# Second query/key groups and half of the mixing linear are placed among 24 uses of score banks

## The reference, cut to what matters

```python
qa, ka, va, qb, kb, vb = even_project(h_lat, w_in, q_gain, k_gain)   # one matrix w_in
qa = apply_rope(qa, cos, sin); ka = apply_rope(ka, cos, sin)
ya, ya_c = global_gqa(qa, ka, va, qa_c, ka_c, va_c, ctx_out)         # the first 8 heads
yb, yb_c = neighbourhood_attention(qb, kb, vb, qb_c, kb_c, vb_c, rpb, ctx_out)  # 8 more
y_lat = jnp.concatenate([ya, yb], -1) @ w_out                        # the mixing linear
x_lat = layer_norm(DN_ALPHA * x_lat + m_lat[2] * y_lat, ...)
```

## Time and profile before

| | |
|---|---|
| three runs | 2612.84, 2616.89, 2617.99 us |
| median | 2616.89 us |
| the profiled execution, first to last instruction | 2617.9 us |
| mean granted clock of TensorE | 0.990 |
| PE busy, DVE busy, ACT busy | 95%, 62%, 49% of the span |
| first to last matmul of the attention and its start of mixing | 147.27 to 261.44 us |

### The profile page before, as it was taken

The page is one execution under the profiler, slowest core; times in us unless marked ns, Lnnn a source line. Parts: engine busy times, 40 slices in busy tenths (PEclk is TensorE's granted clock), DMA queues, the critical chain, the costliest instruction groups (busy, mean ns, idle before and its releaser), DMA issues.

```text
span 2617.9 us, 41421 instructions
## 1 busy us (share of the span) xinstructions
PE 2496.8 (95%) x15930; PEld 2086.0 (80%) x15930; DVE 1616.8 (62%) x2600; ACT 1271.2 (49%) x2348; POOL 253.3 (10%) x266
## 2 busy tenths in 40 slices
PE   7998999999988999999999999899999999999998
PEld 4865778888956999889886687688889899778887
DVE  2646565553677786668776763533325798775664
ACT  3355454433657665544326743422225644675553
POOL 3000100001202100305000001000002430011000
PEclk9999999999999999999999999999999999999999
DMA  8256522224555555534424434532235555634555
GB/s 282 88 207 205 193 89 97 97 88 133 163 167 198 162 183 170 172 119 146 126 93 151 154 124 169 209 96 96 91 94 167 165 182 169 199 115 138 188 176 150
DMA packets 137893, 393.56 MB, mean 150 GB/s; under 512 B 13776, under 2 KB 40400, under 8 KB 137616
## 3 DMA queue, kind: packets, MB, share of 16 engines
q1 hardware_dynamic: 135872, 386.47, 45.9%
q0 software_dynamic: 1872, 5.02, 0.7%
HBM read 390.39 MB, written 1.05 MB: 150 GB/s over the span
## 4 chain that ended last, share of the span: by engine, by line
PE 80%; DVE 8%; ACT 5%; DMA 4%; issue 2%; POOL 1%; SPq 0%; ACTq 0%; DVEq 0%; POOLq 0%
PE bank L722 20%; PE bank L723 20%; PE bank L724 20%; PE bank L719 4%; PE bank L770 2%; DVE w_low L2065 2%; PE bank L718 2%; ACT w_high L1312 1%; PE bank L937 1%; DMA ring<-in_w_mod 1%; PE bank L950 1%; DMA ring<-in_w_down 1%; PE bank L910 1%; PE bank L912 1%; PE bank L911 1%
## 5 line engine op out<-in xcount | busy, mean ns | idle before, releaser
L2065 DVE TENSOR_TENSOR w_low<-ring,w_high 128x1024 fp32r<-128x1024 f32 (+2 forms) x604 | 689.2, 1142 | 519.8 <-ACT w_high L1312 517.4
L722 PE MATMUL bank<-h_high,w_high 128*128 128x512 f32 (+1 forms) x2576 | 883.9, 343 | 36.5 <-DVE h_low L2262 7.9
L724 PE MATMUL bank<-h_high,w_low 128*128 128x512 f32 (+1 forms) x2576 | 869.7, 338 | 0.0
L723 PE MATMUL bank<-h_low,w_high 128*128 128x256 f32 (+1 forms) x2432 | 821.2, 338 | 0.0
L1312 ACT CAST w_high<-ring 128x1024 fp32r<-128x1024 f32 (+2 forms) x604 | 574.1, 953 | 284.2 <-DMA ring<-in_w_down 147.7
L722 PEld LDWEIGHTS bank<-h_high,w_high 128*128 128x128 f32 x2576 | 493.0, 191 | 98.7 <-issue 25.1
L724 PEld LDWEIGHTS bank<-h_high,w_low 128*128 128x128 f32 x2576 | 493.1, 191 | 50.6
L723 PEld LDWEIGHTS bank<-h_low,w_high 128*128 128x128 f32 x2432 | 464.7, 191 | 49.5 <-issue 1.7
L722 PE MATMUL bank<-f_high,w_high 128*128 128x256 f32 (+1 forms) x616 | 194.9, 316 | 4.3 <-DVE w_low L2065 3.8
L724 PE MATMUL bank<-f_high,w_low 128*128 128x256 f32 (+1 forms) x616 | 193.0, 313 | 0.0
L723 PE MATMUL bank<-f_low,w_high 128*128 128x256 f32 (+1 forms) x528 | 168.1, 318 | 0.0
(11 more groups left out here) (323 smaller groups left out, 3515.9 us busy)
## 6 DMA issues: line engine op xcount, KB each, us to landing
ring<-in_w_up SPq DMA_DIRECT2D x176, 512.0 KB, 3.4
ring<-in_w_mod SPq DMA_DIRECT2D x112, 512.0 KB, 4.6
ring<-in_w_down SPq DMA_DIRECT2D x80, 384.0 KB, 3.1
ring<-in_w_down SPq DMA_DIRECT2D x80, 320.0 KB, 3.0
spare_slabs<-in_w_mod SPq DMA_DIRECT2D x48, 512.0 KB, 7.9
ring<-in_w_gate SPq DMA_DIRECT2D x48, 512.0 KB, 3.4
ring<-in_w_k SPq DMA_DIRECT2D x32, 512.0 KB, 3.5
ring<-in_w_v SPq DMA_DIRECT2D x32, 512.0 KB, 3.5
```

The lines of the kernel that those rows point to most:

```text
L722: pe.matmul(out, wh[:, cols], high, start=first, stop=False)
L723: pe.matmul(out, wh[:, cols], low, start=False, stop=False)
L724: ins = pe.matmul(out, wl[:, cols], high, start=False, stop=last)
L2065: v.tensor_tensor(wl[:, cols], raw[:, cols], wh[:, cols].bitcast(F32), ALU.subtract).then_inc(low_ready, 1)
```

## The change

ev_qk is cut: its first 5 groups stay, then ev_v, and the 8 groups for the second heads (ev_qk_b) are done inside the first heads' attention. mix1_0 is cut by rows of w_out: mix1_0_a takes the first heads' 4 chunks (8 groups of 12 matmuls, half slabs of 0.26 MB) inside the second heads' attention, and its product is added to X there; mix1_0 keeps the second heads' 4 chunks. The attention is counted in 24 uses of two score banks each (three banks, 2, 3 and 4, in turn; bank 1 is free for the woven linears). The lists QK_AT, MIX_AT and MODS_AT say at which use a linear's group and how many modulation slabs stand, and SP loads in that order (`Woven`). Head norm and rope of the first heads move under the last ev_qk and the ev_v groups, the masking of the bias moves into uses 2, 5, 7 and 8, and part 1_0_1 is turned and stored at use 12. Probabilities of uses 0 to 11 go to parts of the qk space, outputs of the first heads to other space. Instruction lists of other layers stay as they are.

```diff
+USES = 24
+QK_AT = [3 * c + i for c in range(4) for i in range(2)]
+MIX_AT = list(range(15, 23))
+MODS_AT = [3] + [2] * 11 + [3] * 3 + [1, 2, 2] * 2 + [1, 1, 2]
...
-            plan += [Linear("ev_qk", 13, [8], TOK, "scalar"), Linear("ev_v", 5, [8], TOK, "scalar")]
+            plan += [Linear("ev_qk", 5, [8], TOK, "scalar"), Linear("ev_v", 5, [8], TOK, "scalar")]
+            qk = Linear("ev_qk_b", 8, [8], TOK, "scalar", source="ev_qk", skip=5, bank=1)
+            qk.opens = 1
+            mix = Linear("mix1_0_a", 8, [4], TOK, "scalar", source="mix1_0", bank=1)
...
+            for s in range(USES):
+                entries += [(L, at.index(s)) for L, at in ((qk, QK_AT), (mix, MIX_AT)) if s in at]
+                entries += [next(slabs) for _ in range(MODS_AT[s])]
...
+            def woven_load(L, k):
...
+                sp.wait_ge(slab_done, L.places[k] - (RING - 1))
...
+            def attend_uses(name, beside):
...
+                scores(0)
+                for s in range(A.uses):
+                    if s + 1 < A.uses:
+                        scores(s + 1)
+                    beside(s)
+                    turn(s)
+                    if s:
+                        values(s - 1)
+                values(A.uses - 1)
...
+                        for k in range(first, first + MODS_AT[s]):
+                            if k and k % 16 == 0:
+                                pe.wait_ge(rows_copied, rows_before + k // 16)
+                            mod_slab(BESIDE["block1"][k // 16], k % 16)
...
+                exps(0)
+                for s in range(A.uses):
+                    if s + 1 < A.uses:
+                        exps(s + 1)
+                    cast(s + 1)
+                    beside(s)
+                    copy(s)
...
+                    def next_cast(s):
+                        if s in QK_AT[1:]:
+                            ahead((At(LIN["ev_qk_b"], QK_AT.index(s), QK_AT.index(s) % RING, None), 0))
+                        elif s in MIX_AT:
+                            ahead((At(LIN["mix1_0_a"], MIX_AT.index(s), MIX_AT.index(s) % RING, None), 0))
+                        elif s == USES - 1:
+                            begin(LIN["mix1_0"], ahead, (0,))
...
+                        done = sum(MODS_AT[:s + 1]) // 16
+                        if done > sum(MODS_AT[:s]) // 16:
+                            mod_copy(BESIDE["block1"][done - 1])
...
+                maxima(0)
+                for s in range(A.uses):
+                    normalise(s)
+                    if s >= 2 and A.last(s - 2):
+                        store(A.owner[s - 2])
+                    if s + 1 < A.uses:
+                        maxima(s + 1)
+                    cast(s + 1)
+                    beside(s)
...
```

349 lines of the change are left out of this document (291 added, 58 removed).

## The result

| | before | after |
|---|---|---|
| median of the runs on this chip | 2616.61 us | 2642.62 us (2637.48 to 2645.52) |
| ratio, with 95% interval | 1 | 1.0099 [1.0081, 1.0118] |
| profiled execution, first to last instruction | 2617.9 | 2643.7 |
| end of the last value turn to first matmul of mix1_0 (attention) | 114.2 | 196.8 |
| less the woven matmuls in it (8 x 5.44 + 8 x 2.72 = 65.3) | 114.2 | 131.5 |

A forecast was written before the change was run, and what follows sets the result against it. PE was taken to bound the linears, with 18.8 us excess over work in the attention. 2617.9 - 18.8 + 19.9 + 5.8 = 2624.8 profiled, 2623.8 as median, less 1 for overlap: 2622.8 us (+5.9), range 2611 to 2632.

The forecast's parts named there:

- new waits in the attention: Waits of PE named one by one, from the start through uses 1 to 14 to the end: sum 15.0 us.
- half clock in the attention: PE at 1.2 GHz behind waits: two drops, 3.4 us as before; 5.1 if the wait at use 1 counts too.
- bursts and borders: More bursts of slabs (24 for 15) and 16 more borders of groups in the attention: 0 to 3, taken as 1.5 us.
- excess of before that goes: Attention of 114.2 us less PE's own work of 95.4: 18.8 us, all won if nothing takes its place.
- mixing linear, half clock left out: End of the mixing linear: last gates stand behind late up slabs, residual at T+30.8 for T+25.0; 5.8 us.
- use 1: Second woven group in the attention: its weights are asked for only when group 0 ends, so PE waits 2.0 us.
- use 14: Slab 32 needs second-part rows that ACT copies behind use 15's exponentials and a cast: PE waits 3.9 us.
- end: End of attention: ACT's cast of the first second-half slab in use 22 holds DVE's norming of use 23; 3.4 us.
- DMA keeps up: Rival, mixing linear: up slabs land before PE ends group 6, the 5.8 falls to 0 to 2; 2617 to 2619; chance 0.18.
- Groups cover everything: Rival, uses 14 and 1: those waits and one clock drop go, about 2610 us with a short mixing wait; chance 0.12.
- DVE becomes the bound: Rival, attention uses 2, 5, 8 and 12 to 14: 1 to 2 us at six uses, 2629 to 2633; chance 0.22.
- It does not do what it says: Rival, attention: each woven group waits for its weights by about what it hides; 2615 to 2620 us; chance 0.06.

The follow-up runs named there:

- b: Changed kernel with slabs per use in uses 12 to 20 altered, so slab 31 ends use 14 and slab 32 starts use 15; ratio 1.0072 to the kernel before.
- k: Changed kernel with mixing linear whole, only query/key groups woven, other slabs per use, first mixing slab cast behind the last turned copies; ratio 1.0003.
- h: Changed kernel with mix1_0 one linear of 8 groups of 24 matmuls again, query/key groups still woven; ratio 1.0049 to the kernel before.
- e: Changed kernel with cures for every named wait joined, and casts at uses 3, 6 and 9 put ahead of exponentials and maxima; ratio 1.0058.
- l_up_ahead: As i, but of eleven spare slabs two load behind mixing slab 4, three behind slab 7 and six behind the second up slab; ratio 1.0010.
- d_gate_before_cast: Changed kernel with gate and residual of mix1_0 groups 6 and 7 ahead of cast and w_low of the two up slabs; ratio 1.0075.
- o_qk_only_spread: As l_up_ahead with its slabs per use, but mixing linear whole and only query/key groups woven; ratio 0.9989 to the kernel before.
- g: Changed kernel with the order of d_gate_before_cast, and of eleven spare slabs two loaded behind mixing slab 4, nine behind slab 7; ratio 1.0082.
- j: As g, but both gates and residuals of mix1_0 groups 6 and 7 ahead of both casts of the up slabs; ratio 1.0086.
- i: As e, but casts of uses 3, 6 and 9 behind exponentials and maxima again, and both last gates and residuals ahead of both up-slab casts; ratio 1.0034.
- a: Changed kernel with the second woven query/key group directly behind the first, use 0's three modulation slabs moved into use 1; ratio 1.0082.
- c: Changed kernel with mix1_0's first half-slab cast moved from use 22 behind use 23's turned copies, its w_low behind use 23's norming; ratio 1.0092.
- f: Changed kernel with mix1_0's first slab cast behind use 23's turned copies, its w_low between the last two stores; ratio 1.0065.

## Why the prediction was wrong

Of the signs that would show it wrong one came true: the attention less the woven groups is 131.5 where it should have been near 115. Everything from the first matmul of ev_qk on, against the steps of the prediction:

| term | predicted | measured |
|---|---|---|
| new waits in the attention | 15.0 | 18.7 |
| half clock in the attention | 3.4 | 8.9 |
| bursts and borders | 1.5 | 8.5 |
| excess of before that goes | -18.8 | -18.8 (kept, so that the rest adds up) |
| mixing linear, half clock left out | +5.8 | +7.3 |
| half clock in the mixing linear 2.1, norm longer by 1.2 (half clock 1.7) | 0 | +3.3 |
| ahead of the attention | 0 | -1.9 |
| overlap | -1 | |
| sum | +5.9 | +26.1 |

**Which way, and the chain of reasons: right.** Each wait that I named is there in its place, for the cause named, and the waits for modulation slabs are gone.

**Waits: right in kind, 3.7 short.** Start 1.8 (2.4), use 1 3.35 (2.0), uses 3, 6 and 9 1.8 (2.6), use 7 0.5 (0.7), use 14 4.4 (3.9), end 6.0 (3.4), and 0.8 for a slab that I hadn't counted. Both large misses are a slab's time to land. At use 1 I took 3.0 from the end of a group to its cast and it was 4.4 (issued 112.49, cast 116.87); at the end 1.8 for a half slab alone in the queue and it was 4.9 (issued 283.38, cast 288.27). In b the same half slab took 2.7. Why a transfer of this size takes now 2.7 and now 4.9 is open.

**The clock: the step that failed most.** I kept the 3.4 of before since 1.50 alone had brought no drop, and charged two drops at 1.7; it was 8.9 in the attention and 12.7 in all, 9.3 more. The profiles of all kernels here hold 39 waits of PE of 2.0 us and more between 100 and 345 us, and in or within 1.5 us behind 35 of them began a stretch at 1.2 GHz; at the 278 shorter ones there are five such stretches more (at 1.86 in k, 1.85 in h, 1.31 and 0.96 in e, and at 1.15 and 0.68 close together in the kernel before). And a drop does not always cost 1.7: at the waits of the changed kernel it was 3.1, 3.0, 5.0 and, in the norm, 1.7. So a wait of 4 us is one of 7. The prediction also works the clock out with the wait at use 1 counted, by the Trainium skill, TensorE: Matmul & The Clock Gate, on HAM oscillation. That section states that a wait which lets the clock fall is paid again each time it recurs; whether a wait of 2.0 does so was my addition. The waits at this place were longer, 3.35 to 4.17 us, and each brought a drop, so three drops was the right count in the attention. The 5.1 was still too little, as it kept the price.

**Bursts and borders: the step that failed next, and that none of the cures brings back.** My 95.4 for PE's own work was low, and 1.5 for the new borders lower. It shows in PE's timeline at one woven half group of the changed kernel:

```profile
244.79 1.13 PE L1037 MATMUL bank<-big 64*128 64x512 f32 x4
245.85 0.50 PE L820 MATMUL bank<-o_halves,w_high 128*128 128x512 f32 x1
246.19 0.40 PE L821 MATMUL bank<-o_halves,w_high 128*128 128x512 f32 x1
246.43 0.40 PE L822 MATMUL bank<-o_halves,w_low 128*128 128x512 f32 x1
...
248.51 0.39 PE L822 MATMUL bank<-o_halves,w_low 128*128 128x512 f32 x1
248.83 1.05 PE L871 MATMUL bank<-ring,cvec_padded 128*8 128x256 f32 x16
```

From its first matmul to the next is 0.34, from its last to the slabs 0.32, between 0.23. A half group takes 2.98 where I counted 2.72, a whole one 5.66 for 5.44: 8 x 0.25 + 8 x 0.22 = 3.8. The values of a use alone take 1.02 where two uses in a row took 1.9, 24 x 0.07 = 1.7; slabs in twos 0.49 each for 0.47, 1.0; scores 24 x 1.06 and 0.9 more at their start, where I had 24.5: 1.8; turns take 1.02, 0.5 less in all than I had. That is 7.8 of the 8.5 measured (131.5 - 18.7 - 8.9 = 103.9, less 95.4). l_up_ahead shows the same number with nothing else in it: no half clock, 7.0 of waits, and 176.5 - 65.3 - 7.0 = 104.2 of work. In the kernel before it was 114.2 - 13.3 - 3.4 = 97.5. So PE's own work takes about 6.6 us more in the woven order than it did before, and that eats a third of the 18.8 that I had called excess over work.

**The mixing linear: right mechanism, 1.5 short and a step missed.** Slabs 6 and 7 and the up slabs were cast at T+20.7, T+25.2, T+29.0 and by T+30.7 (T the first matmul), for T+16.7, T+21.1, T+24.9 and T+26.2. Of these 4, 1.5 is the pair of groups that ran at half clock, so that the fifth mixing slab was issued at T+7.0 (305.79) and not at T+5.5; for the rest, the transfers were slower at their start (357 GB/s from 307 to 315, 409 from 315 to 325). What ends the stage is not the last residual but group 6's, with POOL's 2.11 behind it; both stand behind the cast of an up slab, as predicted, and in d_gate_before_cast, where they don't, the wait is gone.

**Head norm 0: right.** The stage ahead of the attention is even 1.9 shorter than 8 groups of 5.44 explain. Half of that is the half clock at its start, which ended at 40.1 for 42.0; the other half I have not traced.

**The rivals.** *DMA keeps up*: wrong, transfers ran at over 400 GB/s from 315 to 325 and casts waited by 3 us. *Groups cover everything*: wrong at both places. *DVE becomes the bound*: wrong; in uses 2 to 13 PE waits for DVE only for w_low, up to 0.89. *It does not do what it says*: this is nearest to what the waits did, but with the half clock and the borders the price was far above what it had.

The theory that stood after the trace, that waits and the half clock behind them are all of the loss, fell in half: cures took 28 us off the sum (307.8 to 279.7), with the ratio still at 1.0010. What is left is the pace, and the mixing half. At equal slabs per use the kernel with both parts woven (l_up_ahead) needs 3.3 us more than with the first alone (o_qk_only_spread), 1.0010 against 0.9989. Of these, 0.9 stand ahead of the attention, where the two kernels are the same and the half clock ended at 41.7 and 39.5. In the attention it is only 0.3 (175.5 less 21.8 for 153.5): the half groups pay 2.0 of borders there and get most of it back, 0.8 of it in shorter waits. The mixing stage is 1.5 longer (26.3 + 21.8 for 46.6) and the norm 0.6, with the same transfers pressed into a shorter stage. Unmended the mixing half costs at most 15.2 (after against h_mixing_whole); the drop at use 14 that h was spared, and the cheaper one at use 1, are 4.7 of that and may be chance.

## What to carry to other kernels

Before work is put into gaps, ask in each place what PE waits for there: uses 15 to 22 waited for nothing, and work that is cut into half groups to fill such a place pays its borders and hides nothing there. On engines whose lists run in order, a cast that waits for its slab holds all that is queued behind it, so place it behind what PE wants next, and put the slab's transfer ahead of bulk transfers; a cure that moves only one of the held steps moves the wait to the next one (d, g, j, i here). In these runs most waits of over 2 us cost their length and 1.5 to 3 us at half clock more, and removing them gave this back too. And when one wait of a profile is cured, look whether the others stayed as they were before the whole gain is put down to the cure: in a, b, c and h a good part of it stood where nothing had been changed.

## What the runs showed of the hardware that I had not expected

- At 35 of 39 waits of PE of 2.0 us or more the clock fell to 1.2 GHz, at a price of 1.4 to 5.1 us. The four exceptions are waits of 2.14, 2.84, 3.05 and 3.35. Just under 2 us it went both ways: waits of 1.91 (b_rows_at_border, last turn) and 1.88 (o_qk_only_spread, first matmul of mix1_0) brought no drop, those of 1.86 (k_qk_only_mended) and 1.85 (h_mixing_whole) at the same first matmul did.
- The same wait in the same order is paid differently: at use 14, up to which c, d, f, g and j share the changed kernel's order, the half clock cost 1.5, 3.0, 3.0, 2.7 and 1.5.
- The first and the last distance of a burst of 512-column matmuls are 0.34 and 0.32 us for 0.23 within it.
- A half slab with little else in the queue took from 2.7 to 4.9 us from issue to cast.
